# A two-block transformer kernel whose first input and side inputs also arrive columns first from the host, with no transposes of them on TensorE

## The reference

```python
h = x                                              # (1, 256, 1024)
mix = dsa_mixer(h, ...)      # proj = x @ w_in: q, k, v, index queries iq, index key ik, weights iw
h = layer_norm(ALPHA * h + mix);  h = layer_norm(ALPHA * h + relu(h @ w_up)**2 @ w_down)
mix = gla_mixer(h, ...)      # then the same norm, MLP, norm
...                                                # second block, on the first one's result
x = layer_norm(ALPHA * x + mla_mixer(x, ...));     x = layer_norm(ALPHA * x + swiglu_ffn(x, ...))
x = x + sigmoid(x @ ple_w_gate[0]) * (p[0] @ ple_w_proj[0])        # p: (2, 1, 256, 256)
x = layer_norm(ALPHA * x + hgrn2_mixer(x, ...));   x = layer_norm(ALPHA * x + swiglu_ffn(x, ...))
x = x + sigmoid(x @ ple_w_gate[1]) * (p[1] @ ple_w_proj[1])
```

## Time and profile before

| what | value |
|---|---|
| median of 3 runs (lowest, highest) | 1242.95 us (1241.42, 1243.8) |
| span of the profiled execution | 1239.5 us |
| PE busy in it | 1229.5 us (99%), 7999 matmuls and transposes |
| DVE / ACT / POOL busy | 853.1 (69%) / 589.4 (48%) / 94.9 us (8%) |
| share of PE in the chain that ended last | 93% |
| HBM read | 218.77 MB, 177 GB/s over the span |

### The profile page before, as it was taken

One profiled execution on the slowest core, in us unless ns is written; L12 is line 12 of the kernel. 1 busy time (PEld: TensorE's weight loads), 2 busy tenths in 40 slices (PEclk: granted clock), 3 DMA queues, 4 the chain that ended last, 5 costly groups with the idle time before them and its releaser, 6 DMA issues.

```text
span 1239.5 us, 18755 instructions
## 1 busy us (share of the span) xinstructions
PE 1229.5 (99%) x7999; PEld 1050.9 (85%) x7999; DVE 853.1 (69%) x919; ACT 589.4 (48%) x712; POOL 94.9 (8%) x226
## 2 busy tenths in 40 slices
PE   9999999999999999999999999999999999999998
PEld 8888888888888888888988888888898888888887
DVE  6887776665775776666776676668587666766675
ACT  5774444334754544334654444345472544444434
POOL 5441000001000200000101000001000100000000
PEclk9999999999999999999999999999999999999999
DMA  8425665655633755654615656555564347655642
GB/s 282 170 69 166 209 197 181 199 187 156 221 115 129 266 183 191 202 175 157 222 60 182 216 181 203 180 194 204 180 191 158 103 150 237 200 186 188 200 141 101
DMA packets 127234, 221.03 MB, mean 178 GB/s; under 512 B 7048, under 2 KB 91296, under 8 KB 127152
## 3 DMA queue, kind: packets, MB, share of 16 engines
q1 hardware_dynamic: 124128, 209.83, 51.0%
q0 software_dynamic: 3024, 10.01, 2.6%
HBM read 218.77 MB, written 1.05 MB: 177 GB/s over the span
## 4 chain that ended last, share of the span: by engine, by line
PE 93%; DVE 3%; ACT 2%; DMA 1%; POOL 1%; issue 1%; SPq 0%; POOLq 0%; DVEq 0%
PE ps L794 20%; PE ps L622 18%; PE ps L796 10%; PE ps L599 10%; PE ps L600 10%; PE ps L601 10%; PE ps L762 4%; PE ps L810 2%; PE ps L706 2%; DVE wlo L1870 1%; PE ps L1034 1%; PE ps L981 1%; DMA raw<-in_ffn_w_in 1%; PE ps L1149 1%; ACT whi L1421 1%
## 5 line engine op out<-in xcount | busy, mean ns | idle before, releaser
L1870 DVE TENSOR_TENSOR wlo<-raw,whi 128x2048 fp32r<-128x2048 f32 (+3 forms) x203 | 452.1, 2241 | 174.6 <-ACT whi L1421 173.4
L1421 ACT ACTIVATE whi<-raw 128x2048 fp32r<-128x2048 f32 (+3 forms) x203 | 376.8, 1869 | 73.0 <-DMA raw<-in_hgrn_w_in 21.7
L794 PE MATMUL ps<-xhl,whi 128*128 128x512 f32 x1088 | 271.8, 392 | 0.0
L794 PEld LDWEIGHTS ps<-xhl,whi 128*128 128x128 f32 x1088 | 198.4, 188 | 37.4
L622 PE MATMUL ps<-whi,xhl 128*128 128x512 f32 (+1 forms) x736 | 182.6, 380 | 0.7 <-ACT xhl L1438 0.6
L599 PE MATMUL ps<-whi,hh 128*128 128x512 f32 x432 | 168.8, 391 | 0.0
L600 PE MATMUL ps<-whi,hl 128*128 128x512 f32 x432 | 168.6, 390 | 0.0
L601 PE MATMUL ps<-wlo,hh 128*128 128x512 f32 x432 | 168.1, 389 | 0.0
L796 PEld LDWEIGHTS ps<-xhl,wlo 128*128 128x128 f32 x1088 | 148.4, 190 | 10.6
L622 PEld LDWEIGHTS ps<-whi,xhl 128*128 128x128 f32 x736 | 130.7, 188 | 26.0 <-issue 0.9
L796 PE MATMUL ps<-xhl,wlo 128*128 128x256 f32 x1088 | 151.7, 282 | 0.0
(11 more groups left out here) (342 smaller groups left out, 1354.8 us busy)
## 6 DMA issues: line engine op xcount, KB each, us to landing
raw<-in_ffn_w_in SPq DMA_DIRECT2D x40, 1024.0 KB, 5.1
raw<-in_mlp_w_up SPq DMA_DIRECT2D x32, 1024.0 KB, 5.4
raw<-in_mlp_w_down SPq DMA_DIRECT2D x32, 1024.0 KB, 4.9
raw<-in_ffn_w_down SPq DMA_DIRECT2D x22, 1024.0 KB, 4.8
raw<-in_hgrn_w_in SPq DMA_DIRECT2D x16, 1024.0 KB, 6.0
raw<-in_b_w_in SPq DMA_DIRECT2D x12, 1024.0 KB, 5.6
raw<-in_ple_w_gate SPq DMA_DIRECT2D x8, 1024.0 KB, 6.0
raw<-in_a_w_in SPq DMA_DIRECT2D x6, 1024.0 KB, 5.8
```

The lines of the kernel that those rows point to most:

```text
L794: mm(bank(b + f), w[0][:, kk, P * f : P * f + P], xhl[:, kk, :, :].rearrange("p a n -> p (a n)"), start=(kk == 0), stop=False)
L1421: a.activation(whi[:, slot, 0:w], raw[:, slot, 0:w], ACT.Copy).then_inc(s["hi_done"], 1)
L1870: v.tensor_tensor(wlo[:, slot, 0:w], raw[:, slot, 0:w], whi[:, slot, 0:w].bitcast(F32), ALU.subtract).then_inc(s["lo_done"], 1)
```

## The change

The host lays x and p out columns first as well: `x_cols` is [128, 8, 256] and `p_cols` two times [128, 512]. The kernel loads `x_cols` in four pieces of two groups of columns (256 KB each), each just ahead of the chunk of `dsa_iq` that uses them, into `buf[6]`. ACT and DVE split it from on-chip memory piece by piece. x, rows first, is still needed by the residual and is now loaded by one DMA of 1 MB behind chunk 5 (`X_BEHIND = 6`: ahead of chunk 6); the first layer norm waits for it. The 16 transposes of x go, and the idle transposes become one run of 40. Products of the first four chunks run over both tiles. p is loaded columns first and split from on-chip memory; its eight transposes go, and with them PE's waits for `p_landed` and `rows_out`.

```diff
@@ sync
-            load_x(0)
+            def load_x_cols(q):
+                sp.dma_start(x_cols[:, 2 * q : 2 * q + 2, :], t["x_cols"][:, 2 * q : 2 * q + 2, :]).then_inc(s[f"x_cols{q}"], 16)
+
+            def load_x():
+                sp.dma_start(x[:, :, :], t["x"][0].rearrange("(t p) d -> p t d", p=P)).then_inc(s["x_landed"], 16)
+
             for n in range(N_CHUNKS):
-                if n == 1:
-                    load_x(1)
+                if n < 4:
+                    load_x_cols(n)
+                if n == X_BEHIND:
+                    load_x()
@@ gpsimd, twice
-            pool.dma_start(ptok, t["p_2"][0, 0].rearrange("(t p) d -> p t d", p=P)).then_inc(s["p_landed"], 16)
+            pool.dma_start(p_cols, t["p_cols"][0]).then_inc(s["p_landed"], 16)
@@ tensor, ffn
-                pe.wait_ge(s["p_landed"], 16 * (layer + 1))
-                pe.wait_ge(s["rows_out"], 2 * ROWS_AT[(T_X5, T_X8)[layer]] + 1)
-                for tt in range(TT):
-                    for q in range(2):
-                        last = nc.tensor.transpose(ps[:, 0, 256 * q + P * tt : 256 * q + P * tt + P], ptok[:, tt, P * q : P * q + P], ident[:, :])
-                last.then_inc(s["p_turned"], 1)
@@ tensor, start
-                            if kk == 0 and q % 2 == 0 and not w_part:
-                                pe.wait_ge(s["turn_lo" if part else "turn_hi"], 2 * tt + q // 2 + 1)
+                            if kk == 0 and tt == 0 and not w_part:
+                                pe.wait_ge(s["x_lo" if part else "x_hi"], q + 1)
-            keep_fed(12)
-            turn_tile(T_X0, x, 0)
-            keep_fed(16)
-            index_queries(0, [0], [HI, LOW_X])
-            turn_tile(T_X0, x, 1)
-            index_queries(0, [0], [LOW_W])
-            index_queries(0, [1], [HI, LOW_X, LOW_W]).then_inc(s["w_done"], 1)
-            for q in range(1, 4):
+            keep_fed(40)
+            for q in range(4):
                 index_queries(q, range(TT), [HI, LOW_X, LOW_W]).then_inc(s["w_done"], 1)
@@ scalar
-                        act.wait_ge(s["p_turned"], layer + 1)
-                        a.activation(hh[:, P_SLOT, :], bank(0), ACT.Copy).then_inc(s["p_hi"], 1)
+                        act.wait_ge(s["p_landed"], 16 * (layer + 1))
+                        a.activation(hh[:, P_SLOT, :], p_cols, ACT.Copy).then_inc(s["p_hi"], 1)
-            turned_tile(T_X0, 0)
-            until(first["dsa_iq"])
-            turned_tile(T_X0, 1)
+            for q in range(4):
+                act.wait_ge(s[f"x_cols{q}"], 16)
+                a.activation(xh[:, 2 * q : 2 * q + 2, :], x_cols[:, 2 * q : 2 * q + 2, :], ACT.Copy).then_inc(s["x_hi"], 1)
+                until(first["dsa_iq"] + q)
@@ vector
+                if i == 0:
+                    dve.wait_ge(s["x_landed"], 16)
-                        v.tensor_tensor(hl[:, P_SLOT, :], bank(0), hh[:, P_SLOT, :].bitcast(F32), ALU.subtract).then_inc(s["p_lo"], 1)
+                        v.tensor_tensor(hl[:, P_SLOT, :], p_cols, hh[:, P_SLOT, :].bitcast(F32), ALU.subtract).then_inc(s["p_lo"], 1)
-            turned(T_X0, 0)
-            until(first["dsa_iq"])
-            turned(T_X0, 1)
-            until(first["dsa_iq"] + 3)
+            for q in range(4):
+                dve.wait_ge(s["x_hi"], q + 1)
+                v.tensor_tensor(xl[:, 2 * q : 2 * q + 2, :], x_cols[:, 2 * q : 2 * q + 2, :], xh[:, 2 * q : 2 * q + 2, :].bitcast(F32),
+                                ALU.subtract).then_inc(s["x_lo"], 1)
+                until(first["dsa_iq"] + q)
@@ module
+X_BEHIND = 6
```

More of the change, by code:

```diff
@@ L106, in build @@
         hl = nc.alloc_sbuf_tensor_at("hl", [P, 4, 512], F32R, offset=buf_home[6])
+        x_cols = buf[6][:, :].rearrange("p (k n) -> p k n", k=KD)
         ident = sb("ident", [P, P])
@@ L225, in build @@
         N_CHUNKS = len(width)
-        (T_X0, T_DSA, T_X1, T_X2, T_GLA, T_X3, T_X4, T_MLA, T_X5, T_X6, T_X7, T_HGRN, T_X8, T_X9) = range(14)
+        (T_DSA, T_X1, T_X2, T_GLA, T_X3, T_X4, T_MLA, T_X5, T_X6, T_X7, T_HGRN, T_X8, T_X9) = range(13)
         ROWS_AT = {T_X1: 0, T_X2: 1, T_X3: 2, T_X5: 3, T_X7: 4, T_X8: 5}
@@ L242, in _ @@
         def _(sp):
-            def load_x(tt):
-                sp.dma_start(x[:, tt, :], t["x"][0, tt * P : (tt + 1) * P, :]).then_inc(s[f"x_landed{tt}"], 16)
-            load_x(0)
+            def load_x_cols(q):
+                sp.dma_start(x_cols[:, 2 * q : 2 * q + 2, :], t["x_cols"][:, 2 * q : 2 * q + 2, :]).then_inc(s[f"x_cols{q}"], 16)
+            def load_x():
+                sp.dma_start(x[:, :, :], t["x"][0].rearrange("(t p) d -> p t d", p=P)).then_inc(s["x_landed"], 16)
             for n in range(N_CHUNKS):
-                if n == 1:
-                    load_x(1)
+                if n < 4:
+                    load_x_cols(n)
+                if n == X_BEHIND:
+                    load_x()
                 src, k, cols = source[n]
@@ L325, in build @@
         warm = sb("warm", [P, 1])
-        ptok = buf[0][:, 0:512].rearrange("p (t c) -> p t c", t=TT)
+        p_cols = buf[0][:, 0:512]
         side = buf[2][:, :].rearrange("p (t c) -> p t c", t=TT)
@@ L580, in _ @@
             pool.wait_ge(s["src_ready"], ready(T_HGRN, 1))
-            pool.dma_start(ptok, t["p_2"][1, 0].rearrange("(t p) d -> p t d", p=P)).then_inc(s["p_landed"], 16)
+            pool.dma_start(p_cols, t["p_cols"][1]).then_inc(s["p_landed"], 16)
             roots(6)
@@ L801, in turn_tile @@
             def turn_tile(j, src, tt):
-                if j == 0:
-                    pe.wait_ge(s[f"x_landed{tt}"], 16)
-                    pe.wait_ge(s["ident_done"], 1)
                 for hf in range(2):
-                    if j > 0:
-                        pe.wait_ge(s["src_ready"], ready(j, tt, hf, j in BY_HALF))
+                    pe.wait_ge(s["src_ready"], ready(j, tt, hf, j in BY_HALF))
                     for q in range(4):
@@ L2488, in ready @@
 def ready(j, tt, hf=1, by_half=False):
-    return 2 * TT * (j - 1) + (TT * hf + tt if by_half else 2 * tt + hf) + 1
+    return 2 * TT * j + (TT * hf + tt if by_half else 2 * tt + hf) + 1
 def vcol0(c):
     return 512 if c == 2 else 0
-INS = ["x", "positions", "a_w_in", "a_w_o", "b_w_in", "b_w_a2", "b_b_a", "b_g_norm", "b_w_o", "ln_mix_g", "ln_mix_b",
-       "mlp_w_up", "mlp_w_down", "ln_mlp_g", "ln_mlp_b", "p_2", "positions_2", "mla_w_dqkv_2", "mla_q_norm_2",
+INS = ["x", "x_cols", "positions", "a_w_in", "a_w_o", "b_w_in", "b_w_a2", "b_b_a", "b_g_norm", "b_w_o", "ln_mix_g", "ln_mix_b",
+       "mlp_w_up", "mlp_w_down", "ln_mlp_g", "ln_mlp_b", "p_cols", "positions_2", "mla_w_dqkv_2", "mla_q_norm_2",
        "mla_kv_norm_2", "mla_w_uq_2", "mla_w_ukv_2", "mla_w_o_2", "hgrn_w_in_2", "hgrn_lb_logits_2",
@@ L2502, with columns_of @@
        "ln_ffn_b_2", "ple_w_proj_2", "ple_w_gate_2"]
+def columns_of(a):
+    return a.T.reshape(-1, P, SEQ).transpose(1, 0, 2)
 def kernel(**inputs):
@@ L2510 @@
     arrays, t = {}, {}
+    inputs["x_cols"] = columns_of(inputs["x"][0])
+    inputs["p_cols"] = np.stack([columns_of(p[0]).reshape(P, 2 * SEQ) for p in inputs["p_2"]])
     for name in INS:
```

## The result

| what | before | after |
|---|---|---|
| median of 8 runs each (lowest, highest) | 1242.55 us (1241.42, 1244.07) | 1245.22 us (1244.53, 1247.37) |
| ratio after / before, 95% interval | | 1.0023 [1.0015, 1.0032] |
| span of the profiled execution | 1239.5 us | 1244.7 us |
| its own device time | | 1246.42 us |

The change costs 2.67 us, 0.23%. The forecast was 1243.4 us, 0.85 us over the median that is now known for the kernel before. A run's own time is 1.7 to 1.8 us above its span in every run that lists both. By that estimate the profiled execution of before took about 1241.2 us, a little under the lowest of its eight runs, while that of after, 1246.42 us, lies above its median.

What follows compares the result with a forecast made beforehand. PE was taken as the bound almost everywhere, with hardly any waits. +1.3 us (wait behind chunk 6) and -0.9 (p) gave +0.4 on the 1239.5 us span, 1239.9; 3.45 us more gave median 1243.4 us, range 1240.4 to 1246.2 us.

Steps and rivals of the forecast that it cites:

- Chunk 6 behind x: Load queue near 21 us: x's 1 MB delays chunk 6 by 2.7 us, less 0.9 for a sooner chunk 5.
- PE is then 1.3 us later than now: PE's transpose of `smallT` waits until about 25.9 us for ACT's copy; the 1.3 us delay is carried to the end.
- my own signs: Wrong if the `smallT` transpose comes before 24.6 us, DMA is under 250 GB/s from 16 to 24 us, or PE's other waits grow.
- Front of PE's stream: Program start: first matmul at 8.69 us, 0.36 later; chunks 0 to 3 end at 20.0 us, 0.5 sooner.
- my claim that it lands as before: Chunk 3's load at the start: the same 1 MB of x is ahead of its end in SP's queue, so it lands as now.
- Side inputs: Transposes of p in both layers: four go in each, 0.44 us each time, -0.88 us in all; bounds -0.88 and 0.
- No wait behind chunk 6: Rival near 22 us: chunk 6 lands by 22.1 us, front's gain stays, -1.4 us, 1241.5 us; chance 0.18.
- DMA slower around x: Rival on x's transfer: at 183 GB/s chunk 6 lands 3.0 us later still, +3.4 us, 1246.4 us; chance 0.10.
- nothing more came back than was counted: Rival without a place: a gain over 2.5 us from an unseen source such as less PSUM contention; chance 0.11.
- Forty idle transposes: Rival in the lead: they leave PE at the slow rate, lead to 10.5 us, +5.0 us, 1248 us; chance 0.04.
- The ending that came: Whole kernel: slower by over 0.2%, chance 0.19; within 0.2% had 0.64, faster 0.17.
- The sum: Whole kernel: +1.3 for PE's delay, -0.9 for p, +0.4 us on a span of 1239.5 us.

Runs made afterwards that it cites:

- half of x: Changed kernel with only tile 0 of x (512 KB) ahead of chunk 6, tile 1 ahead of chunk 10: 1243.6 us, 1.0008.
- filled wait: Changed kernel with 16 idle transposes where PE waits for the copy of `smallT`: 1242.77 us, 1.0002 against the kernel before.
- second profile of the same kernel: Profile from timing the changed kernel again, unaltered: 1244.87 us, 1.0015 against the kernel before.
- lead of 28: Changed kernel with x behind chunk 9 and 28 idle transposes in the lead instead of 40: 1245.9 us, 1.0029.
- x alone: Changed kernel with the hunks on p undone (rows first, eight transposes of p): 1244.36 us, 1.0019 against the kernel before.
- copy first: Changed kernel with ACT's copy of `smallT` ahead of the split of chunk 6, x still ahead of chunk 6: 1243.02 us, 1.0003.
- x late, copy first: Changed kernel with x after chunk 9 and ACT's copy of `smallT` ahead of the split of chunk 6: 1241.79 us, 0.9998.
- three edits: Changed kernel with x after chunk 9, `smallT` copy before chunk 6's split, DVE's low part of chunk 5 before its index-query copy: 1244.0 us, 1.0011.
- two pieces: The kernel with x after chunk 9, `smallT` copy first and DVE reordered, plus x columns loaded in two 512 KB pieces, not four: 1246.73 us, 1.0035.
- side inputs alone: Kernel before with only the hunks on p (columns first, no transposes of p): 1241.3 us, 0.9991.
- lead of 52: Changed kernel with x behind chunk 9 and 52 idle transposes in the lead instead of 40: 1241.79 us, 0.9992.

## Why the prediction was right or wrong

*Chunk 6 behind x.* Right in its path and in size. Forecast: split at 23.4 us, transpose of `smallT` at about 25.9 us, PE 1.3 us late; measured 23.76, 25.99 and 1.42 us. Chunk 6 came 2.2 us later than before: 2.7 us of transfer less 0.5, where I had taken off 0.9 for a sooner chunk 5. SP issued chunk 5 1.5 us sooner (10.9 against 12.4 us), yet it landed at 17.7 us in both traces. Moving x or moving the copy removes the wait, with half of x a third of it is left.

*"PE is then 1.3 us later than now", and nothing more.* This is the step that failed. I priced an idle PE by its length. The clock fell to 0.50 after it, for some 3 us of matmuls, and cost as much again: 1.4 us. The rows of before did not show this: PE's one later wait of that size, 1.2 us near 638 us, left the granted clock at 1.00. The slow rate at the start was a sign of what an idle PE can bring, and I used it for the lead alone. The filled wait shows what brought it: same DMA, same late copy, PE not idle at it, clock at 1.00. By my own signs, too, the prediction failed here: it was to be wrong if PE's other waits grew, and a new one of 1.0 us came for chunk 5 and stops of 2.3 us at L975.

*Front of PE's stream.* In the chain the first product started at 8.05 us, not at 8.69 us, since the rate doubled sooner in that execution; in the second profile of the same kernel it started at 8.95 us. The forecast lies between. PE was done with chunk 3 at 19.0 us, a microsecond before the forecast, and it was worth nothing, as I wrote, but for one more reason than I gave: PE stood still for the low part of chunk 5 until 23.19 us (23.52 before). I had not looked at DVE's chain of angles, copy and split, which sets this time. Before, DVE waited only 0.39 us for PE ahead of that copy, so it could start only about that much sooner (timelines of before and after, one fence each):

```profile
20.58 0.69 DVE L2195 COPY buf<-ps 128x512 f32<-128x512 f32 x1 [0.39 <-PE ps L1034]
```
```profile
20.25 0.68 DVE L2187 COPY buf<-ps 128x512 f32<-128x512 f32 x1
```

Of the 1.5 us that PE had gained in front, 0.33 was left at `dsa_k`. Chunk 3 landed 0.14 us later than before; my claim that it lands as before was near enough.

*Side inputs.* Forecast 0.88 us; alone 1.15 us, with an interval from 0 to 2.1. The traces show 0.3 and 0.2 us in the two layers of the kernel after, 0.3 and 0.5 us alone, where 0.44 us was forecast for each. Inside the whole change the pair of runs does not tell it.

*The rivals.* "No wait behind chunk 6" did not come, "DMA slower around x" neither (404 GB/s), and nothing more came back than was counted. Forty idle transposes did bring the fast rate, with no matmul ahead of it: in 6.47 us at 0.2225 and 0.109 us apiece, about 21 of them were fast. The sentence of the Trainium skill on transposes (TensorE: Matmul & The Clock Gate, "PE-mode transpose"), weighed there, finds no support in any run here, and the 16 idle transposes in the filled wait did not let the clock fall. The ending that came, slower by 0.23%, was given 0.19.

*The sum.* Forecast +0.4 us on the span. By the traces it is +1.4 (wait), +1.4 (clock), -0.5 (p) and +2.8 (the stops at L975), which makes +5.1 of the 5.2 us between them; the medians say +2.67 [+1.9, +4.0], as neither the clock's fall nor the stops are the same in each execution. That the median, 1245.22 us, lies within the stated range of 1240.4 to 1246.2 us is in part luck: the upper end was there for a slower DMA, which did not come, and neither the clock nor the stops were in the sum.

## What to carry to other kernels

Where TensorE otherwise hardly idles, a new wait can cost twice its length: two waits of 1.0 and 1.6 us close together brought a halved clock that cost as much again as the second, in some executions and not in others. A wait that looks the same in the trace of before (1.2 us, clock left whole) does not rule this out. Before a large transfer is put into a queue, look up whose instruction waits for the next one, and what stands behind that instruction on its engine; here a copy of 0.38 us behind a split turned a late weight chunk, needed microseconds later, into a stop of TensorE. If such a wait can't be removed, idle transposes in it may keep the clock, as 16 of them did here in the profile. And a count of idle matmuls at the start is not neutral for what comes later: it shifts the whole stream of TensorE, and the stops told below, which go with it, took up to 4.1 us in a profile (lead of 28), more than the transposes that the change took away.

## What the runs showed that I had not expected

- The clock after a wait is not the same in all executions. Near 25 us it fell in the profile after, with waits of 1.0 and 1.6 us, and in that of x alone, with 1.5 and 0.9 us. It did not in the second profile of the changed kernel (0.25 and 1.4 us), with half of x ahead (1.0 and 0.55 us), nor after a single wait of 1.3 us (copy first) or 1.4 us (x late, copy first). Later in the program it fell after single stops of 2.2 us (three edits), 2.5 us (two pieces) and 2.3 us (lead of 28), and stayed after stops of 2.1 us at L975 (copy first, half of x ahead).
- PE stops for 0.2 to 2.3 us in the middle of a run of 64 small matmuls (L975), with no releaser in the profile, and always at the same place of its stream. In every profile with such a stop, 2101 or 6256 matmuls stand ahead of it, whatever the kernel; the number of small matmuls that are left shifts with the count ahead (timelines of the kernel after, of the lead of 28, and of the side inputs alone):

```profile
336.57 0.44 PE L975 MATMUL ps<-buf 128*32 128x16 f32 x30 [0.83 <-issue]
```
```profile
334.24 0.33 PE L975 MATMUL ps<-buf 128*32 128x16 f32 x18 [1.73 <-issue]
```
```profile
332.95 0.46 PE L974 MATMUL ps<-buf 128*32 128x16 f32 x34 [0.88 <-issue]
```

- How long PE stops there goes with how many small matmuls of the run came just before. With the lead of 28 it is 45 or 46, and both stops are there, 1.73 and 2.33 us. With 33 or 34 (all kernels with 40 ahead) 13 of 17 places have a stop, of 0.21 to 2.09 us. With 25 to 30 (before, side inputs alone, the second place of x alone) it is one of five, and with 17 to 22 (the lead of 52, the filled wait) none of four. This fits the slow median with 28, the narrow spreads with 52 and with the wait filled, and part of the gain of the latter. Whether a stop comes is not set by the count alone: up to 333 us the side inputs alone have PE's program of before, and they have a stop that the profile of before lacks. Why PE stops there no run shows.
- 0.25 MB pieces at the head of the queue moved 136 GB/s from 2 to 4 us, the tiles of 0.5 MB of the kernel before 324.
